# Rotary embedding: the cosine product taken by VectorE on the PSUM bank instead of by GpSimd on a copy

## The reference, cut to what matters

```python
def rope(x, pos):
    d = x.shape[-1]
    half = d // 2
    inv = 1.0 / (ROPE_THETA ** (jnp.arange(half, dtype=jnp.float32) * 2.0 / d))
    ang = pos[:, None] * inv[None, :]
    cos = jnp.cos(ang)[None, :, None, :]
    sin = jnp.sin(ang)[None, :, None, :]
    x32 = x.astype(jnp.float32)
    x1, x2 = x32[..., :half], x32[..., half:]
    return jnp.concatenate([x1 * cos - x2 * sin, x2 * cos + x1 * sin], axis=-1).astype(x.dtype)
...
    for l in range(DEPTH_2):
        h = rmsnorm(x, attn_norm[l])
        z = h @ w_in[l]
        ...
        yA = forgetting_attention(heads(qA, FOX_HEADS), heads(kA, FOX_HEADS), heads(vA, FOX_HEADS),
                                  fA, forget_bias[l])
        yB = dsa_attention(rope(heads(qB, DSA_HEADS), pos), rope(kB[:, :, None], pos)[:, :, 0], vB,
                           rope(heads(qI, IDX_HEADS), pos), rope(kI[:, :, None], pos)[:, :, 0], wI)
        r = retention(rope(heads(qC, RET_HEADS), pos).astype(jnp.float32),
                      (rope(heads(kC, RET_HEADS), pos) * HEAD_DIM ** -0.5).astype(jnp.float32),
                      heads(vC, RET_HEADS).astype(jnp.float32))
        yC = (head_groupnorm(r, ret_norm[l]) * jax.nn.silu(gC.astype(jnp.float32))).astype(x.dtype)
        yD = sliding_window_gqa(rope(heads(qD, SWA_Q_HEADS), pos), rope(heads(kD, SWA_KV_HEADS), pos),
                                heads(vD, SWA_KV_HEADS), attn_sinks[l])
        ...
```

## Time and profile before

| | |
|---|---|
| median of 3 runs | 3462.42 us (3459.98 to 3464.98) |
| the profiled execution's own time | 3458.67 us |
| its span, first to last instruction | 3457.4 us |
| TensorE busy | 3380.0 us, 98% of the span |
| VectorE, ScalarE, GpSimd busy | 1604.8, 1417.9 and 1368.0 us |
| mean granted TensorE clock | 0.995 of full |

### The profile page before, as it was taken

One profiled execution on the slowest core, in us unless ns is written; L12 is line 12 of the kernel. 1 busy time (PEld: TensorE's weight loads), 2 busy tenths in 40 slices (PEclk: granted clock), 3 DMA queues, 4 the chain that ended last, 5 costly groups with the idle time before them and its releaser, 6 DMA issues.

```text
span 3457.4 us, 44415 instructions
## 1 busy us (share of the span) xinstructions
PE 3380.0 (98%) x16880; PEld 2716.6 (79%) x16880; DVE 1604.8 (46%) x3064; ACT 1417.9 (41%) x2397; POOL 1368.0 (40%) x1064
## 2 busy tenths in 40 slices
PE   7999999998999999999999999999999999999998
PEld 5888899885688887877776878887877776788887
DVE  7866566667410115755542343232865452344142
ACT  4223455655432324354443344343354453344242
POOL 2776200021244443434433444444535433444443
PEclk9999999999999999999999999999999999999999
DMA  8566455221132323223222222323323222223332
GB/s 308 199 217 218 128 185 174 87 92 49 43 98 92 100 90 101 89 69 92 86 86 73 92 92 90 106 87 113 100 73 95 80 74 92 92 80 97 98 96 87
DMA packets 117717, 373.27 MB, mean 108 GB/s; under 512 B 15360, under 2 KB 16256, under 8 KB 117120
## 3 DMA queue, kind: packets, MB, share of 16 engines
q1 hardware_dynamic: 115024, 364.74, 32.3%
q10 hardware_dynamic: 2480, 5.68, 0.5%
HBM read 356.73 MB, written 2.10 MB: 104 GB/s over the span
## 4 chain that ended last, share of the span: by engine, by line
PE 88%; DVE 5%; ACT 2%; DMA 1%; issue 1%; POOL 1%; SPq 1%; ACTq 0%; POOLq 0%; DVEq 0%
PE ps L1486 26%; PE ps L1488 26%; PE ps L1487 26%; PE ps L1756 2%; PE ps L1773 1%; PE ps L1738 1%; PE ps L1529 1%; PE ps L1733 1%; DMA b<-b 1%; PE ps L1546 1%; PE ps L1797 1%; PE ps L1808 1%; DVE b L2446 1%; SPq L1417 0%; DMA b<-in_ada 0%
## 5 line engine op out<-in xcount | busy, mean ns | idle before, releaser
L1486 PE MATMUL ps<-b,b 128*128 128x512 f32 (+1 forms) x4688 | 1769.0, 377 | 28.9 <-POOL b L2777 6.7
L1488 PE MATMUL ps<-b,b 128*128 128x512 f32 (+1 forms) x4688 | 1734.6, 370 | 0.0
L1487 PE MATMUL ps<-b,b 128*128 128x512 f32 (+1 forms) x4688 | 1733.3, 370 | 0.0
L2776 POOL TENSOR_TENSOR b<-b,b 128x512 fp32r<-128x512 f32 (+1 forms) x510 | 650.1, 1275 | 2029.5 <-ACT b L1837 2025.9
L1486 PEld LDWEIGHTS ps<-b,b 128*128 128x128 f32 x4688 | 884.3, 189 | 217.1 <-issue 52.9
L1488 PEld LDWEIGHTS ps<-b,b 128*128 128x128 f32 x4688 | 884.3, 189 | 153.5
L1487 PEld LDWEIGHTS ps<-b,b 128*128 128x128 f32 x4688 | 885.3, 189 | 149.1 <-issue 5.5
L1837 ACT ACTIVATE b<-b 128x1024 fp32r<-128x1024 f32 (+1 forms) x618 | 603.6, 978 | 316.7 <-PE ps L1488 307.5
L2777 POOL TENSOR_TENSOR b<-b,b 128x512 fp32r<-128x512 f32 (+1 forms) x510 | 676.2, 1326 | 0.0
L1901 ACT ACTIVATE b<-b 128x512 fp32r<-128x512 f32 (+1 forms) x110 | 64.8, 589 | 346.5 <-DVE b L2322 243.6
L2408 DVE CUSTOM_DVE_ANT_0 b<-b,b,b 128x1024 bf16<-128x1024 f32 x108 | 187.9, 1740 | 39.0 <-DMA b<-in_ada 31.2
(11 more groups left out here) (240 smaller groups left out, 2385.9 us busy)
## 6 DMA issues: line engine op xcount, KB each, us to landing
b<-in_w SPq DMA_DIRECT2D x454, 512.0 KB, 3.4
b<-in_ada SPq DMA_DIRECT2D x86, 512.0 KB, 5.9
b<-in_w SPq DMA_DIRECT2D x80, 384.0 KB, 3.0
b<-in_w SPq DMA_DIRECT2D x80, 320.0 KB, 2.9
b<-b SPq DMA_DIRECT2D x160, 64.0 KB, 2.0
b<-in_const SPq DMA_DIRECT2D x24, 256.0 KB, 3.9
b<-in_x SPq DMA_DIRECT2D x2, 1024.0 KB, 11.4
out<-b SPq DMA_DIRECT2D x8, 256.0 KB, 2.0
```

The lines of the kernel that those rows point to most:

```text
L1486: pe.matmul(out, a[0], b[0], start=first, stop=False, **kw)
L1487: pe.matmul(out, a[0], b[1], start=False, stop=False, **kw)
L1488: return pe.matmul(out, a[1], b[0], start=False, stop=last, **kw)
L2776: pool.tensor_tensor(wlo[j % NS][:, 0:h], raw[j % NR][:, 0:h], whi[j % NS][:, 0:h].bitcast(F32), ALU.subtract)
```

## The change

The cosine product moves from GpSimd to VectorE, which forms it in the PSUM bank, in place, ahead of the sine product. The rotation's sum reads that bank. So the bank is given back by the sum (event `rope`) and no longer by ScalarE's copy (event `ra`), and `number()` holds it until step `rope` part 1. In the changed kernel the lines from 829 on stand one further down, and from the rotation's sine product (2387, now 2391) on four.

```diff
@@ number()
         elif k == "evac":
             t = s["t"]
             name, i, l = t["name"], t["i"], t.get("l")
-            held[t["bank"]] = False
+            held[t["bank"]] = name in ROPES
...
             elif name in ROPES:
-                t["freed"] = ("ra", name, l, i)
+                t["freed"] = ("rope", name, l, i)
                 mark("ra", name, l, i)
...
             if s["part"] == 0:
-                mark("rp", t["name"], t["l"], t["i"])
+                mark("rc", t["name"], t["l"], t["i"])
                 mark("rv", t["name"], t["l"], t["i"])
             else:
+                held[t["bank"]] = False
                 mark("rope", t["name"], t["l"], t["i"])
@@ dve_program()
                 if st["part"] == 0:
+                    b = PB[t["bank"]]
                     at.wait_ge(s["d_cs"], 16 * (l + 1))
+                    at.wait_ge(*n("ra", name, l, i))
+                    dve.tensor_tensor(b[:, :], b[:, :], cos, ALU.mult).then_inc(up("rc", name, l, i), 1)
                     at.wait_ge(s[f"d_half{x % 2}"], 64 * (x // 2 + 1))
                     dve.tensor_tensor(dst[:, i, :], dst[:, i, :], sin, ALU.mult).then_inc(up("rv", name, l, i), 1)
                 else:
                     at.wait_ge(*n("rv", name, l, i))
-                    at.wait_ge(*n("rp", name, l, i))
-                    dve.tensor_tensor(dst[:, i, :], dst[:, i, :], Q[x % 2][:, :], ALU.add).then_inc(up("rope", name, l, i), 1)
+                    at.wait_ge(*n("rc", name, l, i))
+                    dve.tensor_tensor(dst[:, i, :], dst[:, i, :], PB[t["bank"]][:, :], ALU.add).then_inc(up("rope", name, l, i), 1)
@@ pool_program()
-            elif k == "rope" and st["part"] == 0:
-                t = st["t"]
-                name, i, l = t["name"], t["i"], t["l"]
-                x = rope_order.index((name, l, i))
-                behind()
-                at.wait_ge(s["d_cs"], 16 * (l + 1))
-                at.wait_ge(s[f"d_half{x % 2}"], 64 * (x // 2 + 1))
-                then(pool.tensor_tensor(Q[x % 2][:, :], Q[x % 2][:, :], cos, ALU.mult), "rp", name, l, i)
```

More of the change, by code:

```diff
@@ L685 @@
     "dve_z": ("z2", "sz"), "dve_fourier": ("fx",), "dve_decay": ("es", "md"), "dve_group": ("gg",), "dve_pair": ("yo", "yp"),
[1 row of a table removed]
[1 row of a table added]
     "dve_index": ("wi", "sc", "m8"), "dve_forget": ("lf", "lfs", "nF"), "dve_max": ("t1", "mx"), "dve_prob": ("pr",),
     "dve_ret": ("c1v", "rd", "yc", "yg"), "dve_yl": ("nfl", "yl"), "dve_mg": ("mgl",), "dve_out": ("o",),
-    "pool_lo": ("lop",), "pool_rope": ("rp",),
+    "pool_lo": ("lop",),
 }
```

## The result

The changed kernel takes 3514.18 us (median of 4 runs, 3510.66 to 3515.17), the kernel before beside it 3463.70 (4 runs, 3459.98 to 3466.04): a ratio of 1.0149 with a 95% interval of 1.0137 to 1.0160, 50.5 us slower. The profiled execution took 3515.17 us, its span 3513.9; before it was 3458.67 and 3457.4.

The account below looks back on a forecast made before the run. TensorE, busy 98% of the span, was taken as the bound. Waits of 84 - 23 - 10 + 6 - 5 = 52 us plus 7 for the clock gave 59, so 3518 profiled and 3521 us median, range 3487 to 3552.

Parts of the forecast that it names:

- Removed: GpSimd's 40 products: On GpSimd: 40 instructions, 62.7 us, and 38.6 us of waits for transfers go; nothing counted for TensorE's low-half waits.
- Added: the product in place at 0.69: On VectorE: 40 cosine products on PSUM at 0.69 us each, 27.6 us more; VectorE's own sum about even.
- The shortfall of 84 us: At the bank's return: rotated tiles' sums end after TensorE wants the bank, 84 us in 28 tiles of two layers.
- 23 for the quicker rotation: In the rotations: without GpSimd's wait and the contended sum each is 0.8 us quicker, 23 us less over 28.
- 10 for waits that give the next tile time: Within runs of rotated tiles: TensorE's wait gives the next copy and transfers time, 10 us off.
- Settles near 2 us a tile: Within a run, TensorE's waits don't die out: 8.3 us to VectorE's sum against 6.5 between tiles' first matmuls.
- +6 for five banks: At gate tiles: three a layer begin in the bank just filled and wait for ScalarE's read, 6 us more.
- -5 for swallowed waits: On TensorE: waits it already has behind these places, 4.9 us for line 2677, are mostly swallowed, 5 us less.
- +7 for the clock: On TensorE: six to eight waits of 3 us or more halve the clock, 1.7 us each, part returning; 7 us.
- Not slower: Rival: rotations end before the bank comes round, by a shortest chain of 5.9 us; 3457 us, chance 3%.
- Mostly die out: Rival: after a run's first wait later tiles find their bank free, 22 us in two layers; 3484 us, chance 12%.
- The waits grow: Rival: ten or more waits a layer each lower the clock, 3548 us, or 3565 with GpSimd contention; chance 12%.

Follow-up runs that it names:

- e_hold: Kernel before with the changed bank numbering and TensorE waiting for the rotation's sum, GpSimd still forming the cosine product: 3520.04 us, ratio 1.0172.
- e_out: Changed kernel, but for qd and kc the cosine product is written to SBUF and the bank is free with it: 3476.38 us, ratio 1.0039.
- e_copy: Kernel before with the cosine product moved to VectorE, on the SBUF copy behind the transfers, bank still freed by ScalarE's copy: 3459.23 us, ratio 0.9991.
- e_num: Kernel before with only the changed bank numbering (five go round), bank still given back by ScalarE's copy: 3468.48 us, ratio 1.0018.
- e_now: Changed kernel with both parts of the rotation directly behind the tile's copy in the order of steps: 3560.17 us, ratio 1.0285.
- e_split: Changed kernel with two of a tile's four transfers issued by ScalarE behind its copy, two by SyncE: 3517.04 us, ratio 1.0158.
- e_few: As e_copy, but for qi, ki and kd the product is formed on the bank, held until the sum: 3458.90 us, ratio 0.9990.
- e_copy_split: e_copy with a tile's four transfers split between ScalarE and SyncE, no bank held: 3468.22 us, ratio 1.0019.

## Why the prediction was right, and in which terms not

It forecast 3521 us, in a range of 3487 to 3552; 3514.18 came. Its likeliest case (3495 to 3548) is the one that happened, and the mechanism is shown by e_hold and e_out: the hold until the sum costs it, and ending the hold at the product for qd and kc gives 38 of 50 us back. That the total came out 8 us off owes something to luck, since two terms were far off in opposite directions. By its steps:

- **Removed: GpSimd's 40 products.** Right: 1024 instructions, 64.6 us less. Nothing was counted for TensorE's waits for low halves, and they went from 6.7 to 6.0 us.
- **Added: the product in place at 0.69.** Right: 0.696 (691 to 700 ns in all 40), and the sum at 0.685. VectorE did come out even (1604.8 to 1600.2 us), but not by the sum given: that set 20.4 us of waiting against busy time. In busy time the product adds 27.9 us and sum and sine product give back 12.9; the rest is mostly the heads' division by the row sum (line 2677, now 2681), 101.2 before and 85.0 after, which was in no term. It is shorter where only the product has left GpSimd (91.0 in e_copy) and where only the hold was added (89.2 in e_hold), so its cause stays open. The rows decided against the rule of 62 extra cycles for a PSUM source (VectorE: DVE Perf Modes of the Trainium skill, section on the TRN2 errata): a median of 686 ns with one input in PSUM, where a sine product that nothing disturbs takes 0.69 us with both in SBUF.
- **The shortfall of 84 us, less 23, less 10, is 51; 41.0 came.** The total of the three was 10 us too high, and two of its parts were mis-sized in opposite directions. The 23 for the quicker rotation: e_hold has the hold with the slow rotation and waits 48.9 us where the change waits 41.0, so it is worth 8. The 10 for waits that give the next tile time: 84 shrank to 48.9 in e_hold, where GpSimd's product and the order are those of before, so what made TensorE itself later there, waits and half clock, took off up to 35. The two overlap: where the product's start is set by its place behind a head's maxima, what comes earlier in the rotation can be shorter and the sum is no sooner.
- **"Settles near 2 us a tile" inside a run.** Right in kind: behind the first wait of 4.1 us (qd,2) the waits up to the one for kc,3's bank are 1.3 to 2.0 us each. The timeline of qd,1 above shows the pin that the prediction worked out from 8.3 against 6.5: part 0 began behind the maxima and divisions that follow scores issued at 1574.10. From qd,2's first matmul (1568.68) to the end of that sum it is 10.9 us and not 8.3, because the scores came 5.4 us after that matmul in place of 2.8: TensorE ran at half clock in between. A fall of the clock so delays the sum as well as TensorE. The largest waits were named as qd,2, qd,3, vc and qc,3; it was qd,2 and vc (4.1 and 4.6 us), the other two stayed under 2 (qd,3 1.3).
- **+6 for five banks.** Right: 4.7 us of waits in 6 places, and e_num alone costs 6.2 us (0.18%).
- **-5 for swallowed waits.** Right: the 4.9 are gone.
- **+7 for the clock.** Right in direction, low in size: 10.5 us. There were four waits of over 3 us (qd,2 and vc in each layer, all over 4), not six to eight, but each of them was followed by a fall, and three of the four falls lasted 6.8 us, not the 3.4 from which the 1.7 apiece were taken. Of the waits around 2 us one was followed by a fall, the one that ends at 2819.82. The rule of the Trainium skill on idle gaps (TensorE: Matmul & The Clock Gate, section "Why this matters for your kernels") agrees with the long waits; the rival built on it (ten or more falls a layer) fell with the number of such waits.
- **Where:** between the first rotation of a layer and the last, as forecast; the 4.1 us ahead of it are mostly half clock in the first block, in one pair of executions.
- **The rivals.** "Not slower" needed copy to sum in 5.9 us. e_now reaches exactly that, 5.89, and is the slowest of all: it got the chain that short by letting VectorE stand for the transfers, and that price the rival had left out. "Mostly die out" (3484) fell 30 us short: the tiles inside a run went on waiting. "The waits grow" (3548 and more) had the clock three times too dear, and product and sum weren't held up by GpSimd's work: they took 700 and 689 ns at most.

What fell was not in the prediction but in the expectations of e_now and e_split: they took the place in the order to be free to move. Both treated the wait of one tensor as a chain by itself, and forgot the queue behind it on VectorE (e_now), and GpSimd's work beside it and the queue of the engine that issues (e_split and its control).

Left open: the 13 us that e_out still costs match its lists (3.3 + 6.3 + 3.7 and twice 0.5 of waits behind rotations, 4.7 behind gate tiles, less the 4.9 and 2.4 that went, is 11.7), but no kernel took these away one at a time.

## What to carry to other kernels

Ask of every buffer not only who reads it last, but what that reader waits for first: here a bank that was held for a 0.6 us copy is held for a copy, a transfer, two products, a sum and a place in a queue, and 1.5% of the time goes with it. If a product must read PSUM, let it write elsewhere and free the bank with it (e_out), or restrict it to tiles whose bank isn't wanted soon (e_few). Moving the late instruction forward helps only as far as what it waits for is there; the queue behind it pays for the rest. The same holds for an engine that is given transfers to issue: what stands behind them in its queue is late by the issue.

## What the runs showed of the hardware

- A VectorE product that reads and writes the same PSUM bank (fp32, 128x512, second operand in SBUF) takes 691 to 700 ns over 40, median 699, in the kernel after; the sine product from SBUF to SBUF in e_copy, where GpSimd isn't at work beside it, takes 682 to 687.
- The same form with both inputs in SBUF takes 679 to 1786 ns in one line of e_copy_split: up to 687 where GpSimd does nothing beside it, 1753 and more where a subtraction of GpSimd on SBUF runs beside it for 0.6 us or longer (20 of 40). With one input in PSUM it stayed within 676 to 689 ns over 40, also in the 4 places of the kernel after, and the 11 of e_split, where GpSimd ran beside it for that long. The views of one line's instructions (duration ns min/median/max, first and last start), the first of e_copy_split, the second of the kernel after:

```profile
L2397 DVE TENSOR_TENSOR b<-b,b x40: 679/1220/1786, 1351.2 to 2771.7; 128x512 f32<-128x512 f32 x40
```

```profile
L2395 DVE TENSOR_TENSOR b<-b,ps x40: 676/686/689, 1354.5 to 2819.1; 128x512 f32<-128x512 f32 x40
```

- Two 64 KB transfers that ScalarE issues behind its copy hold its queue for 1.16 us, and its next instruction starts 1.24 us after the copy has ended (e_copy_split); four that SyncE issues take 2.41 us (the kernel after).
